# Third attention layer: values as the stationary side, two units on the two halves of a bank, and an output that comes out already turned

## What is computed

```python
q, k, v = split(h @ w_in)              # h: 512 latent and 256 context tokens
out_a = window_attention(...)          # heads 0-7: 2 key/value heads, keys of the own and the
                                       # neighbouring blocks of 128, and all 256 context keys, sinks
out_b = neighbourhood_attention(...)   # heads 8-15: all 512 keys with a bias, and 256 context keys
ctx_out = ctx_self_attention(...)      # 256 context queries on 256 context keys, 16 heads
x = x + gate * (concat(out_a, out_b) @ w_out)
```

## Time and profile before

| | |
|---|---|
| median of three runs | 3796.45 us |
| the three runs | 3794.34, 3796.45, 3812.18 us |
| span of the profiled execution | 3795.4 us |
| TensorE busy | 3681.0 us (97%) |
| TensorE weight loads | 3100.7 us (82%) |
| VectorE busy | 2584.1 us (68%) |
| ScalarE busy | 1439.7 us |
| GpSimd busy | 330.7 us |
| mean granted TensorE clock | 0.994 |

### The profile page before, as it was taken

One profiled execution on the slowest core, in us unless ns is written; L12 is line 12 of the kernel. 1 busy time (PEld: TensorE's weight loads), 2 busy tenths in 40 slices (PEclk: granted clock), 3 DMA queues, 4 the chain that ended last, 5 costly groups with the idle time before them and its releaser, 6 DMA issues. The chain is left out here.

```text
span 3795.4 us, 52487 instructions
## 1 busy us (share of the span) xinstructions
PE 3681.0 (97%) x19210; PEld 3100.7 (82%) x19210; DVE 2584.1 (68%) x4522; ACT 1439.7 (38%) x2574; POOL 330.7 (9%) x460
## 2 busy tenths in 40 slices
PE   8999999999999999999999999999999999999999
PEld 6888777888888877788887899889999878687888
DVE  6667674767766767567676478477777674647887
ACT  4222454222422234542224467333222454534332
POOL 0000021000000001200000011101212100001221
PEclk9999999999999999999999999999999999999999
DMA  6443312433444322134322111021111110002232
GB/s 246 136 135 100 110 35 90 147 130 122 141 138 133 116 72 78 62 117 137 129 89 76 51 57 46 28 78 56 67 67 67 68 47 1 28 24 90 93 106 84
DMA packets 96049, 341.38 MB, mean 90 GB/s; under 512 B 10816, under 2 KB 13248, under 8 KB 95069
## 3 DMA queue, kind: packets, MB, share of 16 engines
q1 hardware_dynamic: 73728, 264.96, 20.6%
q0 software_dynamic: 17152, 63.66, 5.1%
q10 hardware_dynamic: 4956, 9.90, 0.7%
HBM read 335.64 MB, written 7.39 MB: 90 GB/s over the span
## 5 line engine op out<-in xcount | busy, mean ns | idle before, releaser
L268 PE MATMUL ps<-h_hi,w_hi 128*128 128x512 f32 (+1 forms) x2194 | 861.1, 392 | 14.1 <-DVE w_lo L223 7.8
L269 PE MATMUL ps<-h_lo,w_hi 128*128 128x512 f32 (+1 forms) x2194 | 850.0, 387 | 0.0
L270 PE MATMUL ps<-h_hi,w_lo 128*128 128x512 f32 (+1 forms) x2194 | 849.8, 387 | 0.0
L223 DVE TENSOR_TENSOR w_lo<-w_first_raw,w_hi 128x1024 fp32r<-128x1024 f32 x243 | 297.1, 1223 | 312.4 <-ACT w_hi L208 312.2
L208 ACT ACTIVATE w_hi<-w_first_raw 128x1024 fp32r<-128x1024 f32 x241 | 255.0, 1059 | 652.2 <-PE ps L270 645.6
L268 PEld LDWEIGHTS ps<-h_hi,w_hi 128*128 128x128 f32 x2194 | 413.1, 188 | 107.0 <-DVE w_lo L223 12.3
L269 PEld LDWEIGHTS ps<-h_lo,w_hi 128*128 128x128 f32 x2194 | 413.3, 188 | 84.9 <-issue 3.4
L270 PEld LDWEIGHTS ps<-h_hi,w_lo 128*128 128x128 f32 x2194 | 412.9, 188 | 84.6
L268 PE MATMUL ps<-a_hi,w_hi 128*128 128x512 f32 x752 | 292.8, 389 | 6.8 <-DVE x L863 6.8
L270 PE MATMUL ps<-a_hi,w_lo 128*128 128x512 f32 x752 | 291.1, 387 | 0.0
L269 PE MATMUL ps<-a_lo,w_hi 128*128 128x512 f32 x752 | 291.0, 387 | 0.0
(11 more groups left out here) (369 smaller groups left out, 7245.4 us busy)
## 6 DMA issues: line engine op xcount, KB each, us to landing
w_first_raw<-in_w_first SPq DMA_DIRECT2D x213, 512.0 KB, 3.5
w_raw<-in_w_first SPq DMA_DIRECT2D x105, 512.0 KB, 3.4
shared<-in_w_ada POOLq DMA_DIRECT2D x96, 512.0 KB, 4.6
w_first_raw<-in_w_mlp SPq DMA_DIRECT2D x64, 512.0 KB, 3.5
w_raw<-in_w_mlp SPq DMA_DIRECT2D x64, 512.0 KB, 4.1
w_first_raw<-in_w_even SPq DMA_DIRECT2D x16, 512.0 KB, 3.5
near_stage<-in_near POOLq DMA_DIRECT2D x32, 256.0 KB, 2.9
w_first_raw<-in_w_odd SPq DMA_DIRECT2D x16, 512.0 KB, 3.4
```

The costliest lines, as they stand in the source:

```text
L223: dve.tensor_tensor(lo, self.raw(n), hi.bitcast(F32), ALU.subtract).then_inc(self.lo_done, 1)
L268: pe.matmul(out, lhs[0], rhs[0], start=start, stop=False)
L269: pe.matmul(out, lhs[0], rhs[1], start=False, stop=False)
L270: return pe.matmul(out, lhs[1], rhs[0], start=False, stop=stop)
```

## The change

`Attention` gets a further mode, `paired`, used by this layer alone.

- The values become the stationary operand (128 keys x 64 features) and the turned probabilities the moving one (128 keys x 128 queries). The result has 64 features on the partitions and 128 queries along the columns. Two units, u even and u + 1, are done together in the iteration of u + 1, block by block in turn, the first on partitions 0 to 63 and the second on 64 to 127 of the same bank and columns. The four pairs of a group fill the bank, and no transpose of the output is left.
- The inverse sums belong to queries, which now lie along the columns. So VectorE spreads each group's eight inverse sums to 128 x 512 (`reciprocal`, at the iteration of the group's last unit, ahead of that iteration's bias), TensorE transposes this in four pieces (`spread`, ahead of the last pair of the group), ScalarE copies the bank to SBUF, and VectorE multiplies the value bank by it (`scaled`). ScalarE writes the high part from SBUF in one instruction of 512 columns, VectorE the low part (`low`), one iteration later.
- `first_turned` now waits for the groups but the last one.

The core of the diff:

```diff
+                def spread(g):
+                    self.wait(pe, self.widened, g + 1)
...
+                    if g:
+                        self.wait(pe, self.out_done, g)
+                    for j in range(4):
+                        c = slice(128 * j, 128 * j + 128)
+                        m = pe.transpose(ps[:, 7 - g % 2, c], self.paired["inv"][:, c], ident[:, :])
+                    m.then_inc(self.spread_done, 1)
+
+                def pair_of_values(u):
+                    g, last = u // 8, len(units[u]["v"]) - 1
+                    copied(u + 1)
...
+                    if u % 8 == 0 and g:
+                        self.wait(pe, self.spread_copied, g)
+                    for b in range(last + 1):
+                        for k in range(2):
+                            m = pe.matmul(ps[64 * k:64 * k + 64, 6 + g % 2, 64 * (u % 8):64 * (u % 8) + 128],
+                                          units[u + k]["v"][b], tmp["pt"][:, k, 128 * b:128 * b + 128],
+                                          start=(b == 0), stop=(b == last))
+                            if b == last:
+                                m.then_inc(self.pv_done, 1)
...
-                    if u >= 1:
+                    if self.paired:
+                        if u % 8 == 7:
+                            spread(u // 8)
+                        if u % 2:
+                            pair_of_values(u - 1)
+                    elif u >= 1:
                         values(u - 1)
...
                     self.exp(act, u + self.ahead)
+                    if self.paired and u % 8 == 7:
+                        g = u // 8
+                        self.wait(act, self.spread_done, g + 1)
+                        if g:
+                            self.wait(act, self.out_done, g)
+                        act.activation(self.paired["inv"], ps[:, 7 - g % 2, :], ACT.Copy).then_inc(self.spread_copied, 1)
+                    if self.paired and u and u % 8 == 0:
+                        g = u // 8 - 1
+                        self.wait(act, self.out_done, g + 1)
+                        act.activation(self.paired["to"][g][0], self.paired["out"].rearrange("p (c n) -> p c n", c=4), ACT.Copy
+                                       ).then_inc(self.chunk_hi, 1)
...
+                def reciprocal(g):
+                    r = 8 * (g % 2)
+                    sums, inv = tmp["sums"][:, r:r + 8], tmp["inv"][:, r:r + 8]
+                    self.wait(dve, self.exped, 8 * g + 8)
...
+                    dve.reciprocal(inv, sums).then_inc(self.inv_done, 1)
+                    self.wait(dve, self.inv_done, g + 1)
+                    if g:
+                        self.wait(dve, self.out_done, g)
+                    dve.tensor_copy(self.paired["inv"].rearrange("p (h d) -> p h d", h=8),
+                                    inv.rearrange("p (h d) -> p h d", d=1).broadcast_to([128, 8, 64])
+                                    ).then_inc(self.widened, 1)
+
+                def scaled(g):
+                    self.wait(dve, self.spread_copied, g + 1)
+                    self.wait(dve, self.pv_done, 8 * g + 8)
+                    if g:
+                        self.wait(dve, self.chunk_lo, g)
+                    dve.tensor_tensor(self.paired["out"], ps[:, 6 + g % 2, :], self.paired["inv"], ALU.mult
+                                      ).then_inc(self.out_done, 1)
+
+                def low(g):
+                    self.wait(dve, self.chunk_hi, g + 1)
+                    hi, lo = self.paired["to"][g]
+                    dve.tensor_tensor(lo, self.paired["out"].rearrange("p (c n) -> p c n", c=4), hi.bitcast(F32), ALU.subtract
+                                      ).then_inc(self.chunk_lo, 1)
...
                     self.low_queries(dve, u + 3)
+                    if self.paired and u % 8 == 7:
+                        reciprocal(u // 8)
                     self.bias(dve, u + self.ahead, before_unit)
...
-                    if u >= 1 and (u - 1) % 8 == 7:
+                    if self.paired:
+                        if u and u % 8 == 0:
+                            scaled(u // 8 - 1)
+                        if u > 8 and u % 8 == 1 or u == len(units):
+                            low((u + 7) // 8 - 2 if u < len(units) else u // 8 - 1)
+                    elif u >= 1 and (u - 1) % 8 == 7:
                         normalise((u - 1) // 8)
```

More of the change, by code:

```diff
@@ L973, in program, with __init__ @@
         class Attention:
-            def __init__(self, S, tmp, units, groups, turns, q_wide=None, ahead=2, wide_by_act=True, after=None, stack=None, early=0, q_rest=None, zeros=None):
-                self.early, self.zeros = early, zeros
+            def __init__(self, S, tmp, units, groups, turns, q_wide=None, ahead=2, wide_by_act=True, after=None, stack=None, early=0, q_rest=None, zeros=None, paired=None):
+                self.early, self.zeros, self.paired = early, zeros, paired
+                self.spread_done, self.spread_copied = (S("spread"), S("spread_out")) if paired else (None, None)
+                self.widened = S("inv_wide") if paired else None
                 self.q_rest, self.q_twice = q_rest, S("q_twice") if q_rest is not None else None
@@ L1033, in __init__ @@
                     self.turned_by[g] = n
-                self.turn_total = n
+                self.turn_total = len(groups) if paired else n
             def counts(self):
@@ L1229, in values @@
                     m.then_inc(self.pv_done, 1)
+                def spread(g):
+                    self.wait(pe, self.widened, g + 1)
+                    if g == 0 and free:
+                        free(pe)
+                    if g:
[7 more added lines that the diff above has]
+                    copied(u + 1)
+                    if u == 0 and free:
+                        free(pe)
+                    if u % 8 == 0 and g:
[7 more added lines that the diff above has]
+                                m.then_inc(self.pv_done, 1)
                 for u in range(len(units) + 1):
@@ L1303, in vector @@
                 tmp, units = self.tmp, self.units
+                def reciprocal(g):
+                    r = 8 * (g % 2)
+                    sums, inv = tmp["sums"][:, r:r + 8], tmp["inv"][:, r:r + 8]
+                    self.wait(dve, self.exped, 8 * g + 8)
+                    if self.groups[g]["minus_sinks"] is not None:
+                        self.wait(dve, self.sink_done, self.sinks_before[g] + 1)
+                        dve.tensor_tensor(tmp["den"][:, :], sums, tmp["es"][:, :], ALU.add).then_inc(self.den_done, 1)
+                        self.wait(dve, self.den_done, self.sinks_before[g] + 1)
+                        sums = tmp["den"][:, :]
+                    dve.reciprocal(inv, sums).then_inc(self.inv_done, 1)
[17 more added lines that the diff above has]
+                                      ).then_inc(self.chunk_lo, 1)
                 def normalise(g):
@@ L2635, in even_layer @@
                 n_groups = len(units) // 8
[L2636 to L2646, removed]
+                groups = [{"minus_sinks": nsink[:, :] if g % 2 == 0 else None} for g in range(n_groups)]
+                to = []
+                for g in range(n_groups):
+                    hh, hl = xs[g // 8]["h"]
+                    t, c = slice(128 * (g // 2 % 4), 128 * (g // 2 % 4) + 128), slice(4 * (g % 2), 4 * (g % 2) + 4)
+                    to.append((hh[:, c, t], hl[:, c, t]))
+                att = Attention(S, at, units, groups, {}, q_wide, stack=stack, early=1, q_rest=q_rest,
+                                zeros=zeros[:, :], paired={"out": O[:, 0, :], "inv": O[:, 1, :], "to": to})
                 def all_out(eng):
```

## The result

| | before | after |
|---|---|---|
| median | 3800.18 us (4 runs, 3794.34 to 3812.18) | 3834.32 us (4 runs, 3829.91 to 3835.02) |
| span of the profiled execution | 3795.4 us | 3833.1 us |
| ratio after / before, 95% interval | | 1.0087 [1.0069, 1.0105] |

A forecast was written before the change was run, and what follows sets the result against it. TensorE was read as the bound now, a closed loop through VectorE and ScalarE afterwards: 3.1 + 24.2 + 43.9 + 97.3 + 38.4 + 22.4 = 229.3 us against 190.9, +39 us with the first pair, so 3835 us; range 3812 to 3878.

The forecast's parts named there:

- TensorE's 86 us hide a ring: Third layer's attention: transposes, copy, bias, exponential, ScalarE's copy, values and next transposes close a loop; 4.54 us to ScalarE's copy.
- T(u): The probability transposes of unit u on TensorE, from whose start the 4.54 us chain was counted.
- Periods: Time per pair of units: 6.08, 5.49, 4.04 and 2.4 us for six, five, four and two blocks.
- The mode: TensorE's column-half mode for the values: about 0.10 us to enter, 0.20 us to leave.
- The halves: Values of two units run at once on separate column halves: 1.29 us for both, where it was 2.58.
- rival 3: Values: each half's loads stand between its own streams, 0.16 us a record, +21 us, 3856; chance 0.07.
- rival 2: Values: no overlap of the column halves, 2.58 us a pair, +43, 3878 us; chance 0.09.
- The boundaries: Group ends: reciprocal, widened copy, spread and high part delay the values, 22.4 us in all.
- Rival 4: TensorE's clock falls in the idle gaps, for a time above 3880 us; chance 0.03.
- Nothing can run ahead: In the loop, two score rows and two pt buffers let no unit start early: bias(u+2) writes the row T(u) reads.
- rival 1: TensorE stays the bound because the loop has slack: -30, 3766 us; chance 0.05.

The follow-up runs named there:

- e1: Kernel before, with only the third layer's values of two units done together behind the odd unit's copies: 3875.89 us, ratio 1.0217.
- e4: Kernel after, with the even unit's exponential moved behind ScalarE's copy of the odd unit's turned probabilities: 3814.98 us, ratio 1.0046.
- e3: Kernel after, with values unit by unit and both units written to partitions 0 to 63, upper half of the output stale: 3872.35 us, ratio 1.0202.
- e5: Kernel after, without its division: no reciprocal, widened copy, spread or copy of it, and a plain copy for the product: 3819.46 us, ratio 1.0054.
- e9: Kernel after, with odd copy before even exponential, spread behind values, product, high and low parts later, values' wait split: 3790.41 us, ratio 0.9977.
- e2: Kernel after, with the two loops of the values swapped, all of the even unit before the odd unit: 3856.65 us, ratio 1.0159.
- e11: Kernel after, with a pair's values going to the halves two blocks at a time: 3828.76 us, ratio 1.0082.

## Why the prediction was right, point by point

- **TensorE's 86 us hide a ring.** Right, and shown by e1 and e4. The chain from T(u) to the end of ScalarE's copy was 4.54 us in rows 4 and is 4.46 (2231.94 to 2236.40) in the trace after.
- **Periods.** Forecast 6.08, 5.49, 4.04 and 2.4 us for six, five, four and two blocks; measured 5.99, 5.33, 3.97 and 2.2 to 2.8. All but the last a little too long. The mode costs 0.17 us to leave, 0.20 taken. The bracket at 2237.92 names an exponential, but the same 0.17 us stands there in e4 with no releaser (2234.74), and in e1, which has no halves, the next transposes follow without it (2239.87). Entering it costs 0.17 us too where it shows, behind the spread (2242.75), 0.10 taken.
- **The halves.** 24 records in 1.29 us, what I took from L2048 in rows 5; those rows showed row halves, no row showed column halves, and that the figure carried over was an assumption that held. Rivals 2 and 3 are out, and e3 shows that rival 2 would have come at 3872 us, 3878 forecast. The page "TensorEngine Tiling (Array Packing)" of the Trainium skill promises up to twice the speed for a side of at most 64 (Overview, Theoretical Speedup), and on the engine itself this trace agrees, 1.29 against 2.59 us; for the kernel it says nothing. If no load ran under a product of either half, a pair would take at least the 1.9 us of rival 3, an estimate from rows 4. The page "TensorE: Matmul & The Clock Gate" of the Trainium skill, Part 3, says that a load overlaps running products only where the row group differs; these halves share their rows, and the 1.29 us do not agree with it.
- **The boundaries.** Too dear: the steps ahead of the values 15.8 us of the 22.4, measured 11.8 (e5). The widened copy took 0.43 us and not 0.50, and other chains ran beside it: in

```profile
2241.62 0.58 ACT L1304 ACTIVATE arena<-ps 128x512 f32<-128x512 f32 x1
2241.68 0.43 DVE L1361 COPY arena<-inv 128x512 f32<-128x512 f32 x1
...
2242.16 0.42 PEld L1241 LDWEIGHTS ps<-ident,arena 128*128 128x128 f32 x4 [1.58 <-DVE arena L1361]
...
2242.75 1.29 PEld L1253 LDWEIGHTS ps<-arena,vb 128*64 128x64 f32 x24 [0.17 <-issue]
```

  the copy that the values wait for anyway ends at 2242.20, so only the spread's own 0.5 us shows, not 0.7. The high part ahead of the copy costs 0.52 (0.6 forecast).
- **The clock.** Rival 4 came in small, and is the term that the sum had at nothing. By stretch, columns as in rows 1:

```profile
2220.00:2223.00 3.00, 0.99 (x7) 0.70 (x5) 2.93 (x10) 1.87 (x4) 0.94 (x2) 1.00 0.18 29
2223.00:2226.00 3.00, 2.79 (x31) 2.60 (x31) 0.95 (x3) 1.64 (x5) 0.82 (x2) 0.76 0.47 150
2226.00:2229.00 3.00, 3.00 (x16) 2.69 (x14) 2.03 (x7) 0.72 (x3) 0.00 (x0) 0.67 0.00 1
...
2232.00:2270.00 38.00, 28.71 (x269) 24.50 (x268) 25.24 (x87) 23.66 (x55) 3.95 (x10) 1.00 0.12 36
2270.00:2273.00 3.00, 1.35 (x20) 1.35 (x22) 2.36 (x8) 2.93 (x7) 1.60 (x4) 0.90 0.34 93
2273.00:2276.00 3.00, 3.00 (x18) 2.53 (x14) 0.64 (x2) 0.79 (x2) 0.00 (x0) 0.54 0.33 87
...
2294.30:2297.30 3.00, 1.35 (x10) 1.14 (x9) 2.87 (x10) 1.85 (x5) 0.00 (x0) 1.00 0.00 0
2297.30:2300.30 3.00, 2.63 (x30) 2.28 (x31) 1.75 (x8) 2.24 (x6) 0.05 (x1) 1.00 0.00 0
```

  Ahead of each fall TensorE was busy for 1.0 to 1.35 of 3 us, and the clock then went to the lower of its two levels for some 3 us; a third case begins at 2357. But a stretch just as idle at 2294.3 was followed by none, and neither e4 nor e5 has one behind T(3). So little work in 3 us does not decide it alone, and what does stays open. Four pairs took 6.43, 7.26, 7.59 and 7.68 us where their like in e5 take 5.99 to 6.11: 4.8 us in all, 1.6 for each fall. So errors cancel, and that the total came so near is in part luck: T(3) to the projection took 224.9 us and not 229.3, with periods and boundaries some 9 us too long and the clock 5 us too cheap; T(3) itself came 1.2 us late, and 2.4 us of the spans' difference lie behind the projection's first load.
- **"Nothing can run ahead."** This sentence was wrong, though the number did not depend on it. The buffers do tie T(u + 2) to the values, but the longest link, the exponential ahead of a copy that doesn't need it, is an order written by hand. With that order, the boundary and the split wait changed, the same arithmetic is 0.23% faster than the kernel before (e9, 0.14 to 0.32 by the ends of the interval). The 3766 us of rival 1 were not reached: in e9 VectorE is busy 160.5 of the 197.3 us from 2191 to 2388.3. Whether its work or another order's wait holds e9 was not separated.
- Left open: whether the values of a pair could go one iteration later with two more buffers for the turned probabilities; it was not tried.

## What to carry to other kernels

Work taken off the busiest engine is worth what the next loop leaves: follow one unit from the first instruction through every queue it passes and back before counting a saving, and price the wait that pairing adds (here more than all the saved work). When such a loop is found, look in it for links that are there only by the order of an engine's queue: moving one exponential behind one copy it doesn't depend on gave back 16 to 19 us, and moving the steps at the boundaries gave 22 us with the loop shortened but 7 to 9 us with it as it was.

## What the hardware showed that I had not expected

- Where the order changes from one column half to the other once, 0.38 us overlap (some three and a half records of 0.1075 us): six blocks in a row on one half and six on the other keep 0.38 of the 1.30 us (e2), and two by two is as good as one by one (1.34 us in e11, 1.29 in the kernel after).
- Idle times of 1.75 us in every six left the clock at 1.00 (2232 to 2270, TensorE busy 28.7 of 38 us). Each of the three falls in the stage, to 0.54 to 0.76 over 3 us, cost 1.6 us. How busy TensorE was in the 3 us before does not foretell a fall: 1.35 us of work came before one (2270 to 2273) and before none (2294.3 to 2297.3), and in e1 one came behind 2.49 of 3 us:

```profile
2347.00:2350.00 3.00, 2.49 (x22) 2.49 (x23) 0.79 (x4) 1.79 (x4) 0.00 (x0) 1.00 0.00 0
2350.00:2354.00 4.00, 4.00 (x23) 4.00 (x23) 1.84 (x7) 1.01 (x3) 0.00 (x0) 0.57 0.00 0
```

- A record with 64 stationary and 128 moving columns keeps the pace of one with 128 and 64 as long as it stays on one half: 24 records in 2.59 us (e3) and 2.62 us (e1, 2237.25 to the next transposes' first load at 2239.87; its row says 2.75 because the last record's end is modelled).
